# Down weights of a Strassen feed-forward layer in half pieces, with a negation, a bank copy and two additions moved in their queues

## The reference

```python
D_FF = int(math.ceil(8 * D_MODEL / 3 / 256) * 256)          # 2816

def swiglu(h, w_gu, w_down):
    gu = h @ w_gu
    g, u = jnp.split(gu, 2, axis=-1)
    return (jax.nn.silu(g) * u) @ w_down
...
        x = x + swiglu(rms_norm_2(x, ffn_norm[l]), ffn_w_gu[l], ffn_w_down[l])
```

## Time and profile before

| | |
|---|---|
| median of 3 runs | 1955.8 us (1955.07 to 1957.76) |
| profiled execution | 1952.36 us |
| its span, first to last instruction | 1950.6 us |
| TensorE busy | 1883.7 us (97%) |
| VectorE busy | 1450.2 us (74%) |
| ScalarE busy | 1210.0 us (62%) |
| first feed-forward layer, units 1 to 10 and down groups | about 1033 to 1349 us |
| second | about 1625 to 1942 us |

### The profile page before, as it was taken

One profiled execution on the slowest core, in us unless ns is written; L12 is line 12 of the kernel. 1 busy time (PEld: TensorE's weight loads), 2 busy tenths in 40 slices (PEclk: granted clock), 3 DMA queues, 4 the chain that ended last, 5 costly groups with the idle time before them and its releaser, 6 DMA issues.

```text
span 1950.6 us, 26707 instructions
## 1 busy us (share of the span) xinstructions
PE 1883.7 (97%) x10258; PEld 1582.1 (81%) x10258; DVE 1450.2 (74%) x1826; ACT 1210.0 (62%) x1786; POOL 272.4 (14%) x339
## 2 busy tenths in 40 slices
PE   5999999999999999999999999999999999999997
PEld 4668768888888888858889899897777779989896
DVE  6677699998999999872557866869444557776868
ACT  4443268888888888844346655657555546655565
POOL 3111210122211101020011011111011111011011
PEclk9999999999999999999999999999999999999999
DMA  8465579999999999962326686775321225777773
GB/s 302 161 216 195 180 260 372 366 378 376 377 377 365 362 369 369 338 220 74 108 66 157 157 199 169 164 187 146 106 65 53 78 76 110 176 191 190 178 169 115
DMA packets 221004, 415.50 MB, mean 213 GB/s; under 512 B 14762, under 2 KB 95543, under 8 KB 219850
## 3 DMA queue, kind: packets, MB, share of 16 engines
q1 hardware_dynamic: 181296, 343.73, 49.5%
q0 software_dynamic: 31008, 59.38, 15.8%
q10 hardware_dynamic: 8570, 10.64, 1.6%
HBM read 381.30 MB, written 24.65 MB: 208 GB/s over the span
## 4 chain that ended last, share of the span: by engine, by line
PE 71%; DVE 11%; DMA 8%; ACT 5%; issue 4%; POOL 1%; ACTq 0%; POOLq 0%; DVEq 0%
PE ps L448 68%; DVE wlo L393 3%; DMA raw<-in_ffn_w_gu 3%; DMA raw<-sums 3%; ACT whi L363 2%; PE ps L2411 1%; DMA raw<-in_ffn_w_down 1%; DVE sums L286 1%; DVE X L3145 1%; ACT raw L255 1%; PE ps L2438 1%; DMA VR<-in_b_subln 1%; DVE ATl L3127 1%; DVE XN L3157 0%; PE ps L3428 0%
## 5 line engine op out<-in xcount | busy, mean ns | idle before, releaser
L393 DVE TENSOR_TENSOR wlo<-raw,whi 128x1024 fp32r<-128x1024 f32 (+1 forms) x638 | 749.2, 1212 | 136.0 <-ACT whi L363 131.6
L363 ACT ACTIVATE whi<-raw 128x1024 fp32r<-128x1024 f32 (+1 forms) x638 | 639.4, 1046 | 232.5 <-PE ps L448 122.3
L448 PE MATMUL ps<-whi,ATh 128*128 128x512 f32 x308 | 121.0, 393 | 6.3 <-DVE X L3145 6.3
L448 PE MATMUL ps<-wlo,ATh 128*128 128x512 f32 x308 | 120.1, 390 | 0.0
L448 PE MATMUL ps<-whi,ATl 128*128 128x512 f32 x308 | 120.0, 390 | 0.0
L448 PE MATMUL ps<-whi,XT0h 128*128 128x512 f32 x256 | 102.9, 402 | 1.7 <-DVE XT0l L2494 1.7
L448 PE MATMUL ps<-whi,XT1h 128*128 128x512 f32 x256 | 102.8, 402 | 1.5 <-DVE XT1l L2494 1.5
L448 PE MATMUL ps<-hT3h,whi 128*128 128x256 f32 (+1 forms) x352 | 103.6, 294 | 0.6 <-DVE hT3l L445 0.6
L448 PE MATMUL ps<-hT5h,whi 128*128 128x256 f32 (+1 forms) x352 | 103.2, 293 | 0.6 <-DVE hT5l L445 0.6
L448 PE MATMUL ps<-hT3l,whi 128*128 128x256 f32 (+1 forms) x352 | 103.4, 294 | 0.0
L448 PE MATMUL ps<-hT3h,wlo 128*128 128x256 f32 (+1 forms) x352 | 103.4, 294 | 0.0
(11 more groups left out here) (529 smaller groups left out, 4894.0 us busy)
## 6 DMA issues: line engine op xcount, KB each, us to landing
raw<-in_w_expert_gate SPq DMA_DIRECT2D x64, 1024.0 KB, 7.3
raw<-in_w_expert_up SPq DMA_DIRECT2D x64, 1024.0 KB, 8.1
raw<-in_w_expert_down SPq DMA_DIRECT2D x64, 1024.0 KB, 6.9
raw<-in_ffn_w_gu SPq DMA_DIRECT2D x44, 1024.0 KB, 7.5
raw<-in_ffn_w_down SPq DMA_DIRECT2D x16, 1024.0 KB, 9.6
raw<-in_ada_w SPq DMA_DIRECT2D x24, 512.0 KB, 4.8
raw<-in_ffn_w_gu POOLq DMA_DIRECT2D x20, 512.0 KB, 5.9
raw<-sums POOLq DMA_DIRECT2D x20, 512.0 KB, 5.6
```

The source lines that it names most:

```text
L363: e.activation(hi[:, c], x, ACT.Copy).then_inc(self.S("w_hi"), 1)
L393: e.tensor_tensor(lo[:, c], raws[h], hi[:, c].bitcast(F32), ALU.subtract).then_inc(self.S("w_lo"), 1)
L448: return e.matmul(o, l, r, start=start, stop=stop, skip_group_check=True)
```

## The change

1. `quad`: each wide (down) quadrant is split in two pieces, chunks 0 and 1, and the rest; with a = 3 these have 1024 and 512 columns. Both wait for the same transfer. Down pieces use the half places 4 to 9, as up pieces do. `halves` and the plan of `W.ends` follow, and so do `W.index` and `js` (the second half of each piece). TensorE waits for a piece's low part at chunk 0 and at chunk 2.
2. `ffn_act`, unit behind a down group (f = 0): at m = 0 only four pieces are rounded ahead in place of `W.depth`, and `negate_over` of the next unit comes at m = 1, so the copy of the first bank stands ahead of the later roundings.
3. `ffn_act`, down group: `negate_first` behind the rounding and the operand of m = 2; `negate_over` of the following unit ahead of m = 6 in place of behind it.
4. `ffn_vec`, down group: the additions of product 5 ahead of the last operand sum (L3248).

```diff
--- before.py
+++ after.py
@@ -188,9 +188,14 @@
         of = {1: (first, None), 5: (over, 1), 6: ((None, first[1]), 2), 3: (right, None), 7: (first, 3), 2: (low, None), 4: (over, 4)}
         for p in order:
             (i, at), t = of[p]
-            made[p] = self.split(name, i, a, 512 if at is None else 256,
-                                 after=None if t is None else (self.S(f"sum{t}"), (q + 1) * (1 if t == 2 else 16)), at=at)
-        self.quad_of[made[6]] = q
+            after = None if t is None else (self.S(f"sum{t}"), (q + 1) * (1 if t == 2 else 16))
+            if at is None:
+                self.split(name, i, 2, 512, after=after, at=0)
+                made[p] = self.split(name, i, a - 2, 512, after=after, at=1024)
+            else:
+                made[p] = self.split(name, i, a, 256, after=after, at=at * a * 256)
+            if p == 6:
+                self.quad_of.update({j: q for j in (made[6] - 1, made[6])})
         self.done_by[low[0]] = made[4]
         self.quads.append((items, a, made))
         return made
@@ -216,13 +221,12 @@
     def halves(self, j):
 
         i, a, b = self.w[j]
-        if self.at[j] is None:
+        at = self.at[j]
+        if at is None:
             n = a * b // 2
-            raws = self.total(self.quad_of[j]) if i is None else [self.raw[self.raw_of[i][0]][:, h * n:(h + 1) * n] for h in range(2)]
-        else:
-            n = a * b
-            raws = self.total(self.quad_of[j]) if i is None else [self.raw[self.raw_of[i][0]][:, self.at[j] * n:(self.at[j] + 1) * n]]
-        return raws
+            return [self.raw[self.raw_of[i][0]][:, h * n:(h + 1) * n] for h in range(2)]
+        x = self.total(self.quad_of[j], False)[0] if i is None else self.raw[self.raw_of[i][0]]
+        return [x[:, at:at + a * b]]
 
     def wide(self, q):
         return self.quads[q][0][0][1] is None
@@ -660,14 +664,13 @@
                 W.split(f"f{name}{l}", i, 8, 256)
             spare_user[l] = W.last_in(3)
             n = 1
+            W.places = [4, 5, 6, 7, 8, 9]
             for f0, fn in FG:
                 a = fn // 2
-                W.places = [4, 5, 6, 7, 8, 9]
                 while 2 * n < f0 + fn:
                     fu, fg = columns(n)
                     W.quad(f"up{l}", ((fg, 0), (fu, 0), (fg, 1), (fu, 1)), 4, ORDER)
                     n += 1
-                W.places = [0, 1, 2]
                 over, first, right, low = ((W.item(down[:, f0 + k:f0 + k + a, h:h + 512]), None)
                                            for k, h in ((0, 512), (0, 0), (a, 512), (a, 0)))
                 W.quad(f"fd{l}", (first, over, low, right), a, ORDER)
@@ -843,8 +846,9 @@
                 for p in ORDER:
                     name = f"fd{l}.{f0}.{p}"
                     R.plan(name, 2, V_, on=collections.deque(v if p in (5, 3) else y if p == 2 else z))
-                    W.ends[W.index[f"fd{l}"][nd]] = R.full(name, 1)
-                    nd += 1
+                    for j in W.index[f"fd{l}"][nd:nd + 2]:
+                        W.ends[j] = R.full(name, 1)
+                    nd += 2
                 R.turn.extend(v + y + z)
 
         ffn_plan(0)
@@ -2975,16 +2979,16 @@
 
             def product(gi, f0, a, m, p):
                 k = 7 * (gi % 3) + m
-                j = W.index[f"fd{l}"][k]
-                w, x = W.parts(j), [operand(i, k, a) for i in range(2)]
+                js = W.index[f"fd{l}"][2 * k:2 * k + 2]
+                ws, x = [W.parts(j) for j in js], [operand(i, k, a) for i in range(2)]
                 for tb in range(2):
                     b = R.claim(e, f"fd{l}.{f0}.{p}", tb)
                     for kc in range(a):
-                        if tb == 0 and kc in (0, a - 2):
-                            e.wait_ge(*W.half(j, 0 if kc == 0 else 1))
-                            if kc == 0 or m == 1:
-                                e.wait_ge(S("left_lo"), splits(l, gi, m, 0 if m == 1 and kc == 0 else 1))
-                        i = mm3(e, b[:, :], [y[:, kc, tb * P:(tb + 1) * P] for y in x], [y[:, kc, :] for y in w],
+                        if tb == 0 and kc % 2 == 0:
+                            e.wait_ge(*W.lowered(js[kc // 2]))
+                        if tb == 0 and (kc == 0 or m == 1 and kc == a - 2):
+                            e.wait_ge(S("left_lo"), splits(l, gi, m, 0 if m == 1 and kc == 0 else 1))
+                        i = mm3(e, b[:, :], [y[:, kc, tb * P:(tb + 1) * P] for y in x], [y[:, kc % 2, :] for y in ws[kc // 2]],
                                 kc == 0 and p in (1, 5, 2), kc == a - 1)
                     i.then_inc(*R.fill(f"fd{l}.{f0}.{p}", tb))
 
@@ -3056,13 +3060,14 @@
             n = 1
             for gi, (f0, fn) in enumerate(FG, 3 * l):
                 a = fn // 2
-                js = W.index[f"fd{l}"][7 * (gi % 3):7 * (gi % 3) + 7]
+                js = W.index[f"fd{l}"][14 * (gi % 3) + 1:14 * (gi % 3) + 14:2]
                 while 2 * n < f0 + fn:
                     f = 2 * n - f0
                     for m, p in enumerate(ORDER):
                         j = up_pieces(l, n)[m]
-                        W.high(e, j + W.depth(j))
-                        if m == 0:
+                        after_down = f == 0 and m == 0
+                        W.high(e, j + 4 if after_down else j + W.depth(j))
+                        if m == (1 if f == 0 else 0):
                             W.negate_over(e, q + 1)
                         if m == 3 and f < fn - 2:
                             W.negate_first(e, q + 1)
@@ -3081,18 +3086,18 @@
                     q += 1
                 e.wait_ge(S("s_sum"), summed(l, gi, 2))
                 high(gi, f0, a, 1, a - 2)
-                W.high(e, js[2] + 1)
-                W.negate_first(e, q)
                 for m in range(2, 7):
+                    if m == 6 and f0 + fn < 22:
+                        W.negate_over(e, q + 1)
                     W.high(e, js[m] + 1)
                     if m < 5:
                         e.wait_ge(S("s_sum"), summed(l, gi, m + 1))
                     high(gi, f0, a, m)
                     if m == 2:
+                        W.negate_first(e, q)
                         W.negate_total(e, q)
                 q += 1
                 if f0 + fn < 22:
-                    W.negate_over(e, q)
                     W.high(e, js[6] + 3)
                     W.negate_first(e, q)
                     W.negate_total(e, q)
@@ -3244,11 +3249,14 @@
                 e.tensor_tensor(a11, a12, a21, ALU.subtract).then_inc(S("s_sum"), 1)
                 W.low(e, js[3] + 1)
                 low(gi, a, 3)
+                for tb in range(2):
+                    add(f0, 5, tb)
                 e.wait_ge(S("s_sum"), summed(l, gi, 4))
                 e.tensor_tensor(a21, a22, a21, ALU.subtract).then_inc(S("s_sum"), 1)
                 for m in range(4, 7):
-                    for tb in range(2):
-                        add(f0, ORDER[m - 3], tb)
+                    if m > 4:
+                        for tb in range(2):
+                            add(f0, ORDER[m - 3], tb)
                     W.low(e, js[m] + 1)
                     low(gi, a, m)
                 q += 1
```

## The result

The change made the kernel slower: a median of 1976.4 us over 4 runs (1973.3 to 1977.8) against 1956.8 us for the kernel before (4 runs, 1955.1 to 1960.6), a ratio of 1.0109 with a 95% interval of 1.0093 to 1.0125. The profiled execution of after took 1975.1 us. Its lines are numbered four higher than those of before: L452 is the matmul (448 before), L3030 the copy (3026), L3155 `gather` (3150), L259 `negate_over` (255), L290 `add_total` (286), L299 `add_first` (295), L397 the low rounding (393).

The account below looks back on a forecast made before the run. TensorE's waits for VectorE's additions and ScalarE's copies bound the kernel, 19 us within reach. Gains of 7.5 us (first layer) and 1.9 (second), 9.4, less 1.5 for a clock stretch, give 7.9: 1955.8 to 1947.9 us, eight in ten 1939.5 to 1953.5.

Parts of the forecast that it names:

- What bounds the kernel: TensorE, busy 97%, waits in the feed-forward layers for VectorE's additions and ScalarE's bank copy; 19 us within reach.
- All six waits before product 3 of the down groups: TensorE's stalls for VectorE's additions, 6.7 us in all: taken as removed, or 0.15 us left each.
- the four before product 6 behind them: In units right behind down groups, TensorE's stalls for ScalarE's first bank copy, 7.5 us in all, would go.
- the prediction's own signs of being wrong: Product 6 waits for VectorE in down groups beyond one, or a wait for product 5's copy behind down groups.
- What is late next: Negation-to-copy weights chain allows only 2.7, 2.1, 1.0, 0.9 us; much of each stall pair returns one unit later.
- The copy behind a down group: First bank's copy precedes the sum3 wait, ending 2.3 us before need; product 5's copy costs 0 to 0.3 us.
- VectorE blocked: Rival, last unit before a down group: half piece awaiting sum1 delays product 7's sum; 1959.9 us, chance 0.06.
- By the walk: Step-by-step timing from profiled durations: the negation behind a down group ends 7.3 us after the unit's start.
- the first case: First layer's first unit behind a down group, where sum4 lands late: negation ends at 8.3 us, product 5's copy 8.9.
- The moved `negate_first`: In down groups the next transfer is issued 0.7 to 1.7 us later, lands 6 us before its product: costed nothing.
- The prediction's last sentence on what would show it wrong: It fails above all if transfer durations shift with their places; each us on the chain is a TensorE us.
- The chain one unit later: One unit past those behind down groups, product 6 waits 0.8 to 2 us for ScalarE's first bank copy.

Follow-up runs that it names:

- 8: The changed kernel with the next unit's negation back at m = 0 and the down group's `negate_first` back ahead of m = 2: 1937.8 us, ratio 0.9893.
- experiment 1: The changed kernel with one line back, the next unit's negation at m = 0 behind a down group: 1944.6 us, ratio 0.994.
- experiment 9: The changed kernel with only the down group's `negate_first` back in its old place, the unit's negation still at m = 1: 1972.2 us, ratio 1.008.
- 12: The kernel of 8 once more, six runs on another chip: 1941.4 us, ratio 0.9927.
- Experiment 6: The changed kernel with SyncE's two plain loads of units 6 and 10 held until sum1 of units 5 and 9 landed: 1978.8 us, ratio 1.0108.
- 5: The kernel of experiment 1 with the copy of product 5 also ahead of the roundings that wait for sum3 and sum4: 1947.2 us, ratio 0.9948.
- experiment 4: The kernel before with only the two additions of product 5 ahead of the last operand sum: 1951.0 us, ratio 0.997.

## Why the prediction was wrong

**What bounds the kernel** was read rightly, and so was where the stalls stand. All six waits before product 3 of the down groups went (0.14 us is left in one), and the four before product 6 behind them. But in their unit came one of the prediction's own signs of being wrong, a wait for the copy of product 5, four times.

**The step that failed is "What is late next"**, with "The copy behind a down group" ahead of it. I followed the late negation to one place only, the weights' chain up to ScalarE's copy of the next unit's first bank. I did not list what on VectorE waits for its load. In the same unit `add_total`, and the rounding of the next unit's product 5, stand ahead of the two sums that free the banks. The prediction never asked how much room these had (it was 3.9 us, below). I had asked this very question for the last unit before a down group (the rival "VectorE blocked") and not for the first one behind it. That rival names the engine and the kind of wait, in another unit and at 6 in 100.

**When the negation runs.** "By the walk" it was to end 7.3 us after the unit's start (8.3 in the first case). It ended 10.7 us after in the first. In the other three it ended at 8.9, 9.7 and 8.8 us, so the walk was 1.5 to 2.4 us short in all four. Two terms were short. In the first unit sum3 landed 6.5 us after the unit's start (4.5 in before), and three roundings and the negation took the 4.2 us behind it. In the others sum3 landed at 4.2 to 4.3 us, and the negation waited for the rounding of the piece of sum4, which landed at 6.8 to 7.6; the prediction counted sum4 in the first case only. The copy of product 5, put at 0 to 0.3 us, cost 2.57, 0.79, 1.56 and 0.70.

**The moved `negate_first`** of the down group was costed at nothing, since its transfer had about 6 us of cover there. But the transfers behind it moved too: with it alone put back, sum3 of unit 4 landed at 3.0 us in place of 6.4 (experiments 8 and 1) and at 3.3 in place of 6.5 (experiment 9 and after). What this costs in time is not shown, as the intervals of 1, 8 and 12 overlap.

**The transfer's duration.** I kept 5.9 us for a transfer whose issue moved. VectorE needs 3.6 us from the landing of sum1 to the end of the sum of product 7 (1158.06 to 1161.61), and TensorE was ready at 1156.2, so sum1 was due at 1152.6. Issued at 1147.20 with 5.9 us it lands at 1153.1 and costs 0.5 us; with 10.8 us it costs 5.4. In before, product 4 started at 1154.37, and sum1 landed at 1146.90, so by the same 3.6 us it had 3.9 us of room. These are estimates from the two timelines. The change took 3.2 us of that by the later issue, 1.2 because TensorE reached product 4 that much sooner in the unit, and 4.9 by the longer transfer. Experiment 6 bears this out: 6.1 us for the transfer, and 0.8 us for the wait. The prediction's last sentence on what would show it wrong, that the durations shift with their places, was where most of the loss came from, yet I had given it no price. That the negation would leave with the plain loads could be read from the queues: both hang on the piece of sum4, as shown above. The Trainium skill says that the issuing engines are no separate paths but share the same 16 DMA engines (DMA: Bandwidth & Descriptors, Issuing engines are not separate DMA queues). The trace agrees, by 10.8 us against 6.1 us in after and experiment 6 for the same transfer issued 11.0 and 10.6 us into its unit. The 3.2 us that the prediction estimated from the fit of the Trainium skill (same page, Anatomy of one DMA — SWDGE (gpsimd) path) was not seen: the 20 accumulating loads of 512 KB in after took 5.8 to 11.2 us.

**The chain one unit later** was forecast at 0.8 to 2.1 us in each of four places. In after it isn't seen, since TensorE lost more before it. With the negation at m = 0 it came in part: none in 1; 1.8, 0.4, 0.8 and 0.9 us in 5; 0.4 us in 8. So relieved stalls do uncover it. Its size in the change itself stays open, since these kernels negate sooner.

**Half pieces.** I costed them at nothing to a little help. Alone they measured 1.0003. The prediction's walk had them bring the additions of the first down group 1.0 us forward; alone they shortened that stall by 0.2 us, from 1.30 to 1.07. The step that the addition of a bank was held up by the operand sum was right (experiment 4).

**Without the failed step**, that is with the negation at m = 0, the gain was 12.7 us (7.4 to 16.2 by the interval of experiment 1), where 7.9 were forecast for the change. The direction of the rest was right. That the sizes are not far apart is in part luck, since the chain wait that the forecast took off did not come there.

What stays open: how much of the 6.8 and 3.3 us between 1 and 8 or 12 is noise (1944.6 against 1937.8 and 1941.4), which of the two VectorE instructions alone would hold the bank, and why the accumulating transfer gives way so far to a plain load that leaves with it.

## What to carry to other kernels

When an instruction that starts a transfer is moved later, list for each in-order queue everything that waits for its landing, and everything behind those that frees something for the bottleneck; one look at the weights' own consumer isn't enough. And price the transfer anew in its new place: ask which other transfers leave in the same microsecond, and whether the event that releases one releases the other. When a change bundles several orders, time each alone: here one line of it cost 32 us, and the rest with one more line put back was a gain of 0.7 to 1.1%.

## What the runs showed of the hardware that was not expected

A 512 KB accumulating load took 5.85 us when it was issued 2.45 us ahead of two 1 MB plain loads (before), 7.5 us in experiment 1 where it left 4.5 us into the unit, and 10.8 us when they left 0.14 and 0.56 us behind it (after). In experiment 1 it ran beside the two accumulating transfers ahead of it, which landed 6.4 and 8.9 us into the unit. The four of after took 10.7 to 11.2 us, while the first plain load beside each landed in 5.6 to 5.7 us (7.1 to 7.8 us in before, behind an accumulating load that had the head start). So of two that leave together the accumulating one gave way. With the plain loads held back it took 6.1 us (5.9 to 7.2 in the four units), and the next accumulating transfer took 9.8 us (9.2 to 9.8) with them 2 us ahead of it.

The granted clock fell to half for 6.8 us behind each wait of 5.5 to 6.0 us, and for 3.4 us behind the 2.28 and 2.06 us waits of before. It fell behind 1.88 us in experiment 1 too, and did not behind 2.57 us in after, 2.22 us in experiment 6 or 1.82 us in experiment 5. So a wait of about 2 us may or may not cost a clock stretch, and only the profile says which.
